# One tuned kernel: the modulation of its third block in column groups, its weights loaded two stages ahead, and opening weights rounded on ScalarE

## The reference, cut to what matters

```python
mod_lat = (jax.nn.silu(c) @ w_ada[l] + b_ada[l])[:, None, :]
mod_ctx = (jax.nn.silu(c_ctx) @ w_ada[l] + b_ada[l])[None, None, :]
sa, sca, ga, sf, scf, gf = jnp.split(mod_lat, 6, axis=-1)
lam = exp(sum(lambda_q1 * lambda_k1)) - exp(sum(lambda_q2 * lambda_k2)) + lam_init
h = modulate(rmsnorm(x, attn_norm_w[l]), sa, sca)        # h * (1 + scale) + shift
```

## Time and profile before

| | us |
|---|---|
| median of 3 runs (lowest, highest) | 4017.21 (4012.12, 4017.29) |
| the profiled execution | 4017.08 |
| its span, first to last instruction | 4015.3 |
| TensorE busy (matmuls) in the span | 3465.6 (86%) |
| VectorE busy | 2324.0 (58%) |
| ScalarE busy | 1510.0 (38%) |
| mean granted clock of TensorE | 0.916 of full speed |

### The profile page before, as it was taken

One profiled execution on the slowest core, in us unless ns is written; L12 is line 12 of the kernel. 1 busy time (PEld: TensorE's weight loads), 2 busy tenths in 40 slices (PEclk: granted clock), 3 DMA queues, 4 the chain that ended last, 5 costly groups with the idle time before them and its releaser, 6 DMA issues. The chain is left out here.

```text
span 4015.3 us, 47423 instructions
## 1 busy us (share of the span) xinstructions
PE 3465.6 (86%) x16407; PEld 2639.5 (66%) x16408; DVE 2324.0 (58%) x2959; ACT 1510.0 (38%) x1896; POOL 141.7 (4%) x130
## 2 busy tenths in 40 slices
PE   7777998999967788899877977839999999999996
PEld 6545787784445567788742845727777777777774
DVE  4265665429131255455533465427888888888885
ACT  1153331010024431110112134217777777777772
POOL 0000000000000100000000000010000000000001
PEclk9879999999978888699988988959999999999997
DMA  5220222312111100122235201029999999999996
GB/s 169 87 69 32 94 94 80 108 63 104 43 53 42 25 9 1 40 99 97 83 122 215 95 1 40 22 78 419 352 365 349 352 364 352 353 358 357 360 341 225
DMA packets 172321, 653.66 MB, mean 163 GB/s; under 512 B 14953, under 2 KB 82377, under 8 KB 114226
## 3 DMA queue, kind: packets, MB, share of 16 engines
q1 hardware_dynamic: 154370, 605.44, 41.6%
q0 software_dynamic: 7568, 25.70, 1.7%
q10 hardware_dynamic: 10272, 21.02, 1.4%
HBM read 611.02 MB, written 36.77 MB: 161 GB/s over the span
## 5 line engine op out<-in xcount | busy, mean ns | idle before, releaser
L448 DVE TENSOR_TENSOR experts_rest<-experts_weights,experts_leading 128x2048 fp32r<-128x2048 f32 x384 | 874.9, 2285 | 99.9 <-ACT experts_leading L3044 99.9
L3044 ACT CAST experts_leading<-experts_weights 128x2048 fp32r<-128x2048 f32 x384 | 717.6, 1904 | 49.0 <-ACT experts_y L3036 24.8
L454 PE MATMUL psum<-experts_leading,experts_xT_leading 128*128 128x512 f32 x1024 | 412.1, 402 | 50.2 <-DVE experts_rest L448 50.2
L456 PE MATMUL psum<-experts_leading,experts_xT_rest 128*128 128x512 f32 x1024 | 411.4, 402 | 0.0
L455 PE MATMUL psum<-experts_rest,experts_xT_leading 128*128 128x512 f32 x1024 | 410.9, 401 | 0.0
L454 PEld LDWEIGHTS psum<-experts_leading,experts_xT_leading 128*128 128x128 f32 x1024 | 195.5, 191 | 109.1 <-DVE experts_rest L448 64.2
L455 PEld LDWEIGHTS psum<-experts_rest,experts_xT_leading 128*128 128x128 f32 x1024 | 196.3, 192 | 47.1
L456 PEld LDWEIGHTS psum<-experts_leading,experts_xT_rest 128*128 128x128 f32 x1024 | 196.2, 192 | 44.9
L454 PE MATMUL psum<-experts_leading,experts_hidden_leading 128*128 128x512 f32 x512 | 209.4, 409 | 0.0
L456 PE MATMUL psum<-experts_leading,experts_hidden_rest 128*128 128x512 f32 x512 | 203.1, 397 | 0.0
L455 PE MATMUL psum<-experts_rest,experts_hidden_leading 128*128 128x512 f32 x512 | 202.5, 395 | 0.0
(11 more groups left out here) (732 smaller groups left out, 6943.2 us busy)
## 6 DMA issues: line engine op xcount, KB each, us to landing
experts_weights<-in_w_up SPq DMA_DIRECT2D x256, 1024.0 KB, 6.9
experts_weights<-in_w_down SPq DMA_DIRECT2D x128, 1024.0 KB, 7.3
ada_weights<-in_w_ada SPq DMA_DIRECT2D x24, 1024.0 KB, 5.2
expert_rows<-experts_y ACTq DMA_DIRECT2D x66, 256.0 KB, 7.1
merge_first<-in_w_merge SPq DMA_DIRECT2D x16, 768.0 KB, 4.0
merge_weights<-in_w_merge SPq DMA_DIRECT2D x16, 768.0 KB, 4.1
ff_up_first<-in_w_up SPq DMA_DIRECT2D x11, 1024.0 KB, 4.9
ff_up_weights<-in_w_up SPq DMA_DIRECT2D x11, 1024.0 KB, 4.7
```

The lines of the kernel that those rows point to most:

```text
L448: return dve.tensor_tensor(out, src, leading.bitcast(F32), ALU.subtract)
L454: pe.matmul(out, lh, rh, start=start, stop=False)
L456: return pe.matmul(out, ll, rh, start=False, stop=stop)
L3044: act.copy(leading[h % LEADING], place(ring, h)).then_inc(masked, 1)
```

## The change

The modulation becomes one stage. The 16 columns of silu(c) are written into a zeroed tile of 128 x 8 x 32, so that each of the eight chunks has a stationary tile of 32 columns, 30 of them zero. Chunk kk goes to the column group kk mod 4, that is to PSUM partitions 32 (kk mod 4) and on, so a unit is two rounds of four products into one bank. VectorE copies the bank (128x512) to `parts`. Four small products per unit, with `parts` as the stationary operand and two columns of a constant of stripes as the moving one, add up the four groups and turn the result into columns at once; they stand behind the products of the next unit in TensorE's list. The bias and the gains follow at the end, the lambdas lie at the start of the same stage.

The twelve units of weights get eight slots of their own. Four are opened and loaded behind the loads of the `ple` stage, four more behind the context load of the `ln2` stage, and the last four are loaded in the modulation stage itself as slots come free.

In `project` the opening unit's leading part is now cast by ScalarE (`mask_opening`): the first cut ahead of the source's leading parts, the other cuts behind those of the opening section. VectorE only makes the rests of the opening unit. Units of four chunks now have three cuts, chunk 0, chunk 1 and chunks 2 to 3, and are loaded by three DMAs instead of two. This holds for all units of such sections, the cast on ScalarE for the first unit of a stage alone.

```diff
-            self.cuts = [(0, 1), (1, self.chunks)]
+            self.cuts = [(0, 1), (1, 2), (2, 4)] if self.chunks == 4 else [(0, 1), (1, self.chunks)]
...
             @block.scalar
             def _(act):
+                def mask_opening(c):
+
+                    act.wait_ge(landed[0][c], 16)
+                    raw, high = (opening.cut(x, c) for x in (ring[0], leading[0]))
+                    act.activation(high, raw, ACT.Copy).then_inc(masked[0], 1)
+
+                opening = sections[0]
+                if opening.split:
+                    mask_opening(0)
                 for s, parts in to_split:
                     for kk in range(s.kc):
                         act.activation(parts.leading[:, kk, :], s.source[:, kk, :], ACT.Copy).then_inc(source_masked, 1)
+                        if s is opening and kk + 1 == s.kc:
+                            for c in range(1, len(opening.cuts)):
+                                mask_opening(c)
+                if opening.split and isinstance(opening.source, Parts):
+                    for c in range(1, len(opening.cuts)):
+                        mask_opening(c)
...
                         dve.wait_ge(landed[slot][c], (turn + landed0[q][slot][c] + 1) * 16)
-                        leading_bits(dve, high, raw).then_inc(masked[slot], 1)
+                        if only is None:
+                            leading_bits(dve, high, raw).then_inc(masked[slot], 1)
                         dve.wait_ge(masked[slot], n + split0[q][slot])
                         rest_bits(dve, low, raw, high).then_inc(split[slot], 1)
...
+    units = ModulationUnits(k)
+    units.open(k, 4)
+
+    def ada_loads(sp, sem):
+        units.load(sp, range(4))
...
-    gated_products(k, "ple", ..., w_ple)
+    gated_products(k, "ple", ..., w_ple, then=ada_loads)
...
+    units.open(k, 4)
     def ctx_load(sp, sem):
         landed = sem("ctx_landed")
         sp.dma_start(cx[:, :, :], k.dram["ctxT"].rearrange("(k p) t -> p k t", p=P)).then_inc(landed, 16)
+        units.load(sp, range(4, 8))
         sp.wait_ge(landed, 16)
...
+def modulation(k, mod, gains, subln, signs, units):
...
+            @block.sync
+            def _(sp):
+                for u in range(held, N):
+                    sp.wait_ge(multiplied, u - held + 1)
+                    units.load(sp, [u])
...
+                def turn(u):
+                    pe.wait_ge(copied, u + 1)
+                    for n in range(4):
+                        spot = 4 * BANK + 2 * (4 * u + n)
+                        last = pe.matmul(k.psum[:, spot:spot + 2], parts[:, u % 2, n * P:(n + 1) * P], k.c("striped")[:, 0:2],
+                                         start=True, stop=True)
+                    last.then_inc(turned, 1)
+
+                pe.wait_ge(opened, 1)
+                for u in range(N):
+                    w = units.slots[u % held]
+                    pe.wait_ge(units.landed[u % held], 16 * (u // held + 1))
+                    if u >= 2:
+                        pe.wait_ge(copied, u - 1)
+                    for kk in range(KD):
+                        j = kk % STRIPES
+                        last = pe.matmul(k.psum[j * STRIPE:(j + 1) * STRIPE, u % 2 * BANK:(u % 2 + 1) * BANK], silu[:, kk, :],
+                                         w[:, kk * BANK:(kk + 1) * BANK], start=(kk < STRIPES), stop=(kk >= STRIPES))
+                    last.then_inc(multiplied, 1)
+                    if u:
+                        turn(u - 1)
+                turn(N - 1)
...
+                for u in range(N):
+                    dve.wait_ge(multiplied, u + 1)
+                    if u >= 2:
+                        dve.wait_ge(turned, u - 1)
+                    dve.tensor_copy(parts[:, u % 2, :], k.bank(u % 2)).then_inc(copied, 1)
...
+                dve.wait_ge(turned, N)
+                dve.tensor_tensor(mod[:, :, :], k.psum[:, 4 * BANK:4 * BANK + 12 * KD].rearrange("p (n c) -> p n c", c=2),
+                                  k.p("b_ada").unsqueeze(2).broadcast_to([P, 6 * KD, 2]), ALU.add).then_inc(biased, 1)
```

More of the change, by code:

```diff
@@ L54 @@
 SEMAPHORES = (100, 170)
-EARLY = (242, 244, 246)
+EARLY = (242, 245, 248)
+ADA = 160
 class Core:
@@ L569, in project @@
         ring = [first.slot if first and i == 0 else sb(f"weights{i}", [P, size]) for i in range(2)]
-        landed = [first.landed if first and i == 0 else [sem(f"weights{i}_half{c}_landed") for c in range(2)] for i in range(2)]
+        landed = [first.landed if first and i == 0 else [sem(f"weights{i}_cut{c}_landed") for c in range(3)] for i in range(2)]
         if first:
@@ L2516, in lay_out_second @@
     p["conv_dw"] = columns(i["conv_dw_2"][0].reshape(-1))
[L2521 to L2546, removed]
-                                      k.p("b_ada").unsqueeze(2).broadcast_to([P, 6 * KD, 2]), ALU.add).then_inc(biased, 1)
@@ L2550, in third_columns, with __init__, open, load @@
-def third_columns(k, mod, gains, subln, signs):
-    nc = k.nc
-    with k.stage("third_columns") as (sb, sem):
-        prod, exps, diff = sb("products", [P, 2]), sb("exps", [P, 2]), sb("difference", [P, 1])
-        own, summed, exped = sem("vector_steps"), sem("sums_ready"), sem("exps_ready")
+class ModulationUnits:
+    def __init__(self, k):
+        self.weights, size = k.dram["w_ada"], KD * BANK
+        above = 4 * (KD + 4) * P + 4 * KD * BANK + 4 * PLE // P * T
+        self.belows = [above + 4 * size * n for n in range(4)] + [4 * KD * CTX] + [above + 4 * size * n for n in range(4, 7)]
+        self.slots, self.at, self.size = [], [], size
+        self.landed = [k.nc.alloc_semaphore(f"ada_unit{n}_landed", num=ADA + n) for n in range(len(self.belows))]
+    def open(self, k, count):
+        for _ in range(count):
+            n = len(self.slots)
+            self.slots.append(k.high(f"ada_unit{n}", [P, self.size], self.belows[n]))
+            self.at.append(k.places[-1])
+    def load(self, sp, units):
+        for u in units:
+            n = u % len(self.slots)
+            sp.dma_start(self.slots[n][:, :], self.weights[u, :, :]).then_inc(self.landed[n], 16)
+    def retire(self, k):
+        k.retired += self.landed
+        for at_ in self.at:
+            k.places.remove(at_)
@@ new lines, in modulation @@
+def modulation(k, mod, gains, subln, signs, units):
+    nc, N = k.nc, 12
+    with k.stage("ada") as (sb, sem):
+        silu, parts = sb("silu", [P, KD, STRIPE]), sb("parts", [P, 2, BANK])
+        prod, exps, diff = sb("products", [P, 2]), sb("exps", [P, 2]), sb("difference", [P, 1])
+        own, summed, exped, cleared, opened, multiplied, copied, turned, biased = (sem(x) for x in (
+            "vector_steps", "sums_ready", "exps_ready", "silu_cleared", "silu_ready", "unit_multiplied", "parts_copied",
+            "parts_turned", "modulation_ready"))
+        units.retire(k)
+        held = len(units.slots)
@@ new lines, in _ @@
+            @block.tensor
+            def _(pe):
+                pe.wait_ge(own, 1)
+                pe.matmul(k.bank(5, 2), k.c("ones"), prod[:, :], start=True, stop=True).then_inc(summed, 1)
+                def turn(u):
[19 more added lines that the diff above has]
+                turn(N - 1)
@@ L3162, in third_block @@
         subln, signs = sb("subln", [P, 1]), sb("signs", [P, 2])
-        modulation(k, mod)
-        third_columns(k, mod, gains, subln, signs)
+        modulation(k, mod, gains, subln, signs, units)
         with ExitStack() as attend:
```

50 lines of the change are left out of this document (28 added, 22 removed).

## The result

The changed kernel takes 3944.9 us (median of 4 runs, 3943.3 to 3955.0) against 4015.9 us before (4 runs, 4012.1 to 4017.3): a ratio of 0.9827, 95% interval 0.981 to 0.9844. The forecast was 3949 us in a range of 3940 to 3975. The profiled execution took 3943.41 us, of which the span is 3941.2, against 4015.3.

What follows compares the result with a forecast made beforehand. Bound by stages in series: TensorE's products alone in the third block's modulation, and six stalls at projection starts. 61.0 us from the modulation plus 6.8 from the openings, 67.8 off 4017.1, gave 3949 us, range 3940 to 3975.

Steps and rivals of the forecast that it cites:

- Start and end of the modulation: Third block's modulation: product starts at 2079.8, 5.4 us earlier; bias, three gains and barrier take 1.1 us at the end.
- Products: Modulation: four column groups run at once, 0.86 us a round, 1.72 us a unit, 20.7 us for twelve units.
- turn: Modulation: four small products per unit, 0.82 us by the first projection's gates, 9.8 us in all.
- change of form: Modulation: TensorE switches between 32-column and full form 24 times, taken at 0.1 us each, 2.4 us; upper bound 6.5 us.
- rival (b): Modulation: groups overlap incompletely at 512 columns (3956 us), or weights come at the experts' rate (3953 us); chance 0.15.
- (c): Modulation: the column groups run one behind another, making the kernel slower, 4042 us; chance 0.03.
- Clock: Modulation: TensorE starts at a clock of 0.50 and spends 5 us at half speed, 2.5 us lost.
- rival (a): Modulation: the clock stays low, TensorE's chain takes 61.1 us instead of 35.4, kernel 3975 us; chance 0.12.
- Weights: Modulation: at 423 GB/s the last unit lands by 2108 and would end at 2113, 3 us before TensorE's chain.
- The openings: Projection starts: six TensorE stalls, 9.97 us, go; later starts through ScalarE's cast cost 3.2 us; net 6.8 us won.
- Rival (d): Projection starts: something else ends last when the stall goes, 3.2 us lost instead of 6.8 won, 3959 us; chance 0.05.
- The sign that the next norm's first square would come near 2112: After the modulation: 2116 less some 4 us from the openings ahead of it.

Runs made afterwards that it cites:

- paired turns: Changed kernel with the turns of two units done together, 12 changes between 32-column and full form instead of 24: 3942.6 us, ratio 0.9819 to the kernel before.

## Why the prediction was right, and where it was not

**Start and end of the modulation.** The product was forecast 1.6 us after the table load; it came 2078.16 - 2076.59 = 1.57 us after it. Behind the last turn 1.1 us were forecast; from 2113.8 to 2114.76 it is 0.96.

**Products, turn, change of form.** Forecast 1.72 + 0.82 + 0.2 = 2.74 us a unit, measured 2.84. The change of form was the term without a row, taken at 0.1 of bounds 0 and 0.27; measured 0.113 us. The products of a unit take 1.71 us between the paired copies, so the round of four groups at 512 columns is 0.86 us as forecast: fourfold, as the rows of 128 columns had it. That leaves 2.84 - 0.23 - 1.71 = 0.90 us for the turn against 0.82: the row of the gates was some 10% too fast for it. The Trainium skill, "TensorEngine Tiling (Array Packing)", Key Properties, has a change of tiling mode drain TensorE; the trace agrees that it costs something, but 0.11 us is less than the 0.27 us of a record run out, by which the sum would have been 4 us longer. The Trainium skill, "TensorE: Matmul & The Clock Gate", Measured speedup vs the span model, gives 2.38 times for three column groups and 3.07 for four row groups at 512 columns; here, with four column groups of fp32, a unit's products took 1.71 us against 6.87 without groups: 4.0 times. The first half of rival (b) falls with that, and (c) with it.

**Clock.** Forecast 5 us at half speed, 2.5 lost. The first unit took 3.7 us (2078.16 to 2081.86) and the second 1.75: it was up after 3.7 us, some 1.8 lost. It stayed at 1.00 through all small products; rival (a) falls. The terms 0.1 us too small for each unit and 0.7 too large for the clock nearly cancel: TensorE's chain 35.4 us forecast, 35.6 measured. So 60.97 against 61.0 is partly luck, though no term is off by more than 1.2 us.

**Weights.** Forecast: not the limit. TensorE waits for no unit, so the second half of (b) falls too. What the loading ahead is worth the experiment without it shows: 31 us.

**The openings.** Forecast 9.97 us of stalls won, 3.2 lost by later starts, net 6.8; measured 6.2 as the mean over kernels, 4.6 in the first profile. The start was later by 0.42 us instead of 0.37 in the seven stages, and by 0.29 instead of 0.1 in the latent one. By stages (forecast, mean of seven kernels less mean of the two with the old opening): first projection -0.3, -0.6; first output -1.45, -0.8; feed-forward +0.5, +0.6; second projections -1.5, -1.0 and +0.4, +0.5; second output -1.4, -1.2; third projection -1.3, -2.0; latent +0.1, +1.5; third output -1.7, -3.2. The mechanism was right, and the stages scatter about it by 1.5 us where the clock moves. In the third output projection the stall cost more than its 2.11 us: behind it the clock was 0.50, and at the same place of the changed kernel it is 1.00 (first row before, second after):

```profile
2568.30:2571.60 3.30, 3.30 (x10) 0.50 0.00 0
...
2502.50:2505.80 3.30, 3.30 (x16) 1.00 0.00 0
```

What the step did not see is that the two edits in it are separate: VectorE's load with a short second cut (0.69 + 1.23 behind the source's rests) could have been summed from the earlier trace rows and the prediction's 4.82 us for those rests: 335.4 + 1.92 + 4.82 + 1.92 = 344.1, where TensorE needs it at 345.5. Rival (d) falls; the 3.2 us of later starts are real but are ScalarE's, not the cuts'.

The sign that the next norm's first square would come near 2112 did not come true, it came at 2114.76: the stretches ahead of the modulation gave 1.6 us (2078.20 - 2076.59) where some 4 were forecast.

**What the sum left out.** 74.1 us of span went, 61.0 + 4.6 are accounted for; 8.5 us came in stages that the change does not touch. So the forecast's 3949 us came within 4 us of the median although the openings gave 2.2 us less than forecast in this profile: other stages more than filled the gap, and no term of the sum stood for them. The largest is the attention behind the latent projection, 84.2 us before and 80.8 after. First the kernel before, then the changed one: TensorE alone over the end of the latent projection and over a stretch of that attention, then over two short parts of the stretch (busy us and records, clock, DMA share, GB/s), and two rows of ScalarE's exponentials behind those parts:

```profile
2460.90:2467.90 7.00, 3.79 (x13) 1.00 0.05 20
2482.90:2507.90 25.00, 19.74 (x96) 0.86 0.00 1
...
2486.40:2489.70 3.30, 3.30 (x4) 0.50 0.00 0
2496.60:2499.90 3.30, 3.30 (x12) 0.50 0.00 0
...
2493.53 0.94 ACT L1115 ACTIVATE mla_probs<-mla_masked,mla_top 128x768 f32<-128x768 f32 x1 [6.17 <-DVE mla_top L1067]
...
2504.55 0.94 ACT L1115 ACTIVATE mla_probs<-mla_masked,mla_top 128x768 f32<-128x768 f32 x1 [7.48 <-DVE mla_top L1067]
```

```profile
2397.30:2404.30 7.00, 4.22 (x10) 0.76 0.01 3
2419.30:2444.30 25.00, 19.74 (x109) 1.00 0.00 1
...
2424.00:2427.30 3.30, 3.30 (x12) 1.00 0.00 0
2434.20:2437.50 3.30, 3.30 (x16) 1.00 0.00 0
...
2429.39 0.94 ACT L1133 ACTIVATE mla_probs<-mla_masked,mla_top 128x768 f32<-128x768 f32 x1 [4.47 <-DVE mla_top L1085]
...
2438.74 0.94 ACT L1133 ACTIVATE mla_probs<-mla_masked,mla_top 128x768 f32<-128x768 f32 x1 [5.81 <-DVE mla_top L1085]
```

The stage starts at 2471.77 before and at 2409.33 after. The same instructions run at a clock of 0.86 in one and 1.00 in the other, because the clock falls to 0.50 in two stretches of the kernel before. Each costs 1.7 us: ScalarE's first row shown comes 2493.53 - 2471.77 = 21.76 us after the stage's start before and 20.06 after, the second 32.78 and 29.41, and nothing is lost behind it. So the two stretches are the 3.4 us. In the changed kernel such a stretch lies at the end of the latent projection instead, whose clock falls from 1.00 to 0.76 and which gets 1.1 us longer in this profile, 1.5 in the mean of the seven; that is the latent stage's miss above.

The seven kernels with three cuts all on ScalarE have 80.7 to 81.0 us in this attention, and so has the one with three cuts on VectorE (80.8); the three with two cuts have 84.1 to 84.2, the two with VectorE in the opening and paired turns 84.4 and 84.5, and the one with the first cut on VectorE 82.4. The clock's stretches at 0.50 behind the one that all have at the stage's start go with it: none, two, two and one. The repetition of the changed kernel shows both windows at 0.76 and 1.00 again, but it is one repetition, and other stages of the same two executions differ (the third of the second block's projections 74.2 and 73.3 us). What decides where the clock falls is not shown. The rest of the 8.5 us is spread and has no cause here; the largest shares are the router's stages -1.5, the experts -2.0 and the last stages -1.4 us, against +2.4 in the sparse attention of the first block.

## What to carry to other kernels

A faster computation can run into the next limit: the overlapped products alone won 29.6 us and then waited for weights, and loading them ahead gave the other 31. Price both limits (85 us of products, some 60 of loading) before leaving one out. When an edit has two halves, sum each half alone against the stall: here the finer cut alone removed it, and the move to the other engine, beside it, only cost. And below some 5 us read stage lengths of several kernels, since a median does not show them and one profile has clock dips of the same size.

## What the runs showed of the hardware

A change between the 32-column form and the full form costs TensorE 0.11 us, measured from both sides (4, 2 and 1 changes a unit: 3.065, 2.84, 2.725 us). Four column groups with fp32 and 512 columns overlap 4.0 times (1.71 against 6.87 us for the same sixteen records). A stage that waits for weights again and again can run at a mean clock of 0.71 (over 68 us, with 18.9 us of waits), where the clock had been up after 3.7 us without them; while the queue brought a unit every 4.90 us this showed in busy time, 34.1 us instead of 24.6 for 192 records, and not in the pace. Two stretches at a clock of 0.50 in an attention stage cost 1.7 us each. Kernels that differ only in stages far ahead can have them or not: with three cuts on VectorE that attention took 80.8 us, and with paired turns besides, 84.5.
